# A split-float matmul kernel: high products of both halves first, then the low products of both halves

## What is computed

```python
def second_block(x, ...):
    for layer in range(2):
        if layer == 0:                                   # chunked attention with a relative bias
            h = rms_norm(x, a_norm)
            q, k, v, g = split(h @ a_w_in, 4)
            o = chunked_relbias_attention(q, k, v, a_rel_bias)
            x = x + (o * silu(g)) @ a_w_out
        else:                                            # attention with cumulative log forget gates
            h_kv = rms_norm(x, kv_norm)
            k, v = split(h_kv @ kv_w, 2)
            decay = cumsum(log_sigmoid(h_kv @ f_w + f_b))
            q, g = split(rms_norm(x, b_norm) @ b_w_in, 2)
            o = forgetting_attention(q, k, v, decay)
            x = x + (o * silu(g)) @ b_w_out
    return rms_norm(x, final_norm)
```

## Time and profile before

| | us | |
|---|---|---|
| median of three runs | 2486.72 | 2486.25 to 2486.83 |
| the profiled execution | 2486.6 | its span is 2484.9 |
| recurrence and what is ahead of it | 0 to 487.8 | TensorE busy 470.6 |
| output projection | 487.8 to 579.4 | TensorE busy 91.1 |
| layer 0 and layer 1 | 579.4 to 2430 | TensorE busy 1849.5 of 1850.6 |
| last projection and norm | 2430 to 2484.9 | TensorE busy 46.4 |

### The profile page before, as it was taken

One profiled execution on the slowest core, in us unless ns is written; L12 is line 12 of the kernel. 1 busy time (PEld: TensorE's weight loads), 2 busy tenths in 40 slices (PEclk: granted clock), 3 DMA queues, 4 the chain that ended last, 5 costly groups with the idle time before them and its releaser, 6 DMA issues.

```text
span 2484.9 us, 43962 instructions
## 1 busy us (share of the span) xinstructions
PE 2457.6 (99%) x16586; PEld 2187.6 (88%) x16586; DVE 1754.9 (71%) x2629; ACT 1219.4 (49%) x1811; POOL 304.0 (12%) x397
## 2 busy tenths in 40 slices
PE   8999999999999999999999999999999999999998
PEld 7999999888888888888888888888888888888887
DVE  8988797996767566666666668667576756666676
ACT  6555333665544444444534456544444444444445
POOL 1212114422100000000000001111010001000011
PEclk9999999999999999999999999999999999999999
DMA  7666763486576666666666665767667766766673
GB/s 216 173 160 170 196 183 87 111 225 189 162 193 187 191 175 181 184 173 193 175 193 186 175 174 167 194 186 185 191 171 190 193 184 182 189 180 181 189 194 102
DMA packets 758308, 442.79 MB, mean 178 GB/s; under 512 B 28784, under 2 KB 721136, under 8 KB 758160
## 3 DMA queue, kind: packets, MB, share of 16 engines
q1 hardware_dynamic: 752880, 430.16, 61.8%
q0 software_dynamic: 5280, 10.56, 3.2%
HBM read 437.35 MB, written 3.31 MB: 177 GB/s over the span
## 4 chain that ended last, share of the span: by engine, by line
PE 95%; DVE 3%; issue 1%; DMA 0%; ACT 0%; POOL 0%; SPq 0%; DVEq 0%; ACTq 0%
PE bank L288 40%; PE bank L294 20%; PE bank L269 5%; PE bank L270 5%; PE bank L271 5%; PE bank L318 5%; PE bank L319 5%; PE bank L320 5%; PE bank L1851 1%; PE bank L1870 1%; PE bank L1858 1%; PE bank L1850 1%; PE bank L1871 1%; DVE lob L253 0%; DMA rawa<-in_w_in_dram 0%
## 5 line engine op out<-in xcount | busy, mean ns | idle before, releaser
L253 DVE TENSOR_TENSOR lob<-rawb,hib 128x1024 fp32r<-128x1024 f32 x672 | 834.6, 1256 | 377.1 <-ACT hib L246 371.0
L246 ACT ACTIVATE hib<-rawb 128x1024 fp32r<-128x1024 f32 x672 | 701.4, 1055 | 515.5 <-PE bank L294 368.0
L288 PE MATMUL bank<-xx,hib 128*128 128x512 f32 x3328 | 842.7, 395 | 0.5 <-DVE xx L2126 0.3
L288 PEld LDWEIGHTS bank<-xx,hib 128*128 128x128 f32 x3328 | 601.5, 189 | 110.5 <-DVE xx L2126 0.9
L294 PEld LDWEIGHTS bank<-xx,lob 128*128 128x128 f32 x3328 | 459.8, 190 | 32.8
L294 PE MATMUL bank<-xx,lob 128*128 128x256 f32 x3328 | 487.3, 285 | 0.0
L269 PE MATMUL bank<-xh,hia 128*128 128x258 f32 (+2 forms) x1040 | 301.7, 290 | 10.7 <-DVE loa L253 10.5
L270 PE MATMUL bank<-xl,hia 128*128 128x258 f32 (+2 forms) x1040 | 296.5, 285 | 0.0
L271 PE MATMUL bank<-xh,loa 128*128 128x258 f32 (+2 forms) x1040 | 295.8, 284 | 0.0
L288 PE MATMUL bank<-oo,hib 128*128 128x512 f32 x1008 | 256.7, 393 | 0.0
L269 PEld LDWEIGHTS bank<-xh,hia 128*128 128x128 f32 x1040 | 197.3, 190 | 15.6 <-DVE loa L253 10.7
(11 more groups left out here) (294 smaller groups left out, 2260.4 us busy)
## 6 DMA issues: line engine op xcount, KB each, us to landing
rawb<-in_a_w_in_dram SPq DMA_DIRECT2D x256, 512.0 KB, 4.7
rawa<-in_w_in_dram SPq DMA_DIRECT2D x130, 512.0 KB, 5.4
rawb<-in_kv_w_dram SPq DMA_DIRECT2D x128, 512.0 KB, 4.5
rawb<-in_b_w_in_dram SPq DMA_DIRECT2D x128, 512.0 KB, 5.2
rawb<-in_a_w_out_dram SPq DMA_DIRECT2D x64, 512.0 KB, 5.1
rawb<-in_b_w_out_dram SPq DMA_DIRECT2D x64, 512.0 KB, 5.0
rawb<-in_w_out_dram SPq DMA_DIRECT2D x32, 512.0 KB, 4.8
table<-in_rel_dram POOLq DMA_DIRECT2D x32, 128.0 KB, 4.0
```

The source lines that it names most:

```text
L246: nc.scalar.activation(self.hi[(2 * at.u + h) % SPL][:], self.raw_half(at, h), ACT.Copy).then_inc(hi_ready, 1)
L253: nc.vector.tensor_tensor(self.lo[b][:], self.raw_half(at, h), self.hi[b][:].bitcast(F32), ALU.subtract).then_inc(lo_ready, 1)
L288: nc.tensor.matmul(out, self.hi[b][:, k * P:(k + 1) * P], both(k).rearrange("p a t -> p (a t)"), start=start and k == 0, stop=False)
```

## The change

`product_wide` and `wide`, which work through one half (8 high products, then 8 low ones), become `pair_wide`, which takes both halves of a unit: the high products of half 0, those of half 1, the low products of half 0, those of half 1. `half_used` is counted up after each half's low products, as before. All wide units go through it: the output projection of the first block, q, k and g of every head, and the projections, where the wait for the bank's last use (`taken`) is made once for both halves. The places of the attention work are written anew. In q_b and k_b it stood before the first high tile of half 1 and now stands before high tile 4 of half 1; in g_a and g_b it stood before low tile 3 of half 0 and now stands before high tile 1 of half 1; the second weighing stood before low tile 3 of half 1 and now stands before low tile 2 of it. In the first unit of each projection the wait for the neighbouring bank stays ahead of half 1's first high tile, which now comes right after six high tiles of half 0. The very last unit keeps its order.

```diff
-        def product_wide(self, pe, at, h, out, both, start, stop, tiles=range(8), before={}):
-
-            b = (2 * at.u + h) % SPL
-            pe.wait_ge(hi_ready, at.count(2 * at.u + h + 1, 2))
-            for k in tiles:
-                if ("hi", k) in before:
-                    before["hi", k]()
-                nc.tensor.matmul(out, self.hi[b][:, k * P:(k + 1) * P], both(k).rearrange("p a t -> p (a t)"),
-                                 start=start and k == 0, stop=False)
-            pe.wait_ge(lo_ready, at.count(2 * at.u + h + 1, 2))
-            for k in tiles:
-                if ("lo", k) in before:
-                    before["lo", k]()
-                last = nc.tensor.matmul(out[:, 0:SEQ], self.lo[b][:, k * P:(k + 1) * P], both(k)[:, 0], start=False,
-                                        stop=stop and k == 7)
-            if k == 7:
-                last.then_inc(half_used, 1)
+        def pair_wide(self, pe, at, outs, both, starts, stops, tiles=range(8), before={}):
             for h in range(2):
+                b = (2 * at.u + h) % SPL
+                pe.wait_ge(hi_ready, at.count(2 * at.u + h + 1, 2))
+                for k in tiles:
+                    if ("hi", h, k) in before:
+                        before["hi", h, k]()
+                    nc.tensor.matmul(outs[h], self.hi[b][:, k * P:(k + 1) * P], both(h, k).rearrange("p a t -> p (a t)"),
+                                     start=starts[h] and k == 0, stop=False)
+            for h in range(2):
+                b = (2 * at.u + h) % SPL
+                pe.wait_ge(lo_ready, at.count(2 * at.u + h + 1, 2))
+                for k in tiles:
+                    if ("lo", h, k) in before:
+                        before["lo", h, k]()
+                    last = nc.tensor.matmul(outs[h][:, 0:SEQ], self.lo[b][:, k * P:(k + 1) * P], both(h, k)[:, 0],
+                                            start=False, stop=stops[h] and k == 7)
+                if k == 7:
+                    last.then_inc(half_used, 1)
+
+        def unit_wide(self, pe, at, xx, before={}):
+
+            wait(pe, taken[at.bank()], at.free())
+            self.pair_wide(pe, at, [GB[at.bank()]] * 2, lambda h, k: xx[:, 8 * h + k], (True, False), (False, True),
+                           before=before)
...
-                for h, (n, rows) in enumerate(out_parts(v)):
-                    if (v, h) == (2, 0):
-                        pe.wait_ge(turned_taken, 2 * (NT - 1))
-                        turn_last()
-                    before = {}
+                at, tiles = out_unit(v), out_parts(v)
+                if v == 2:
+                    pe.wait_ge(turned_taken, 2 * (NT - 1))
+                    turn_last()
+                if tiles[0][0] >= EARLY:
+                    wait(pe, taken[at.bank()], at.free())
+                before = {}
+                for h, (n, rows) in enumerate(tiles):
                     if rows is rows_a:
-                        pe.wait_ge(ya_low, 1)
-                        before = {("hi", 4): lambda: pe.wait_ge(xlo_ready, 2)}
-                    a_first = CT if rows is rows_a else 0
-                    if n < EARLY:
-                        st.product_wide(pe, out_unit(v), h, out_bank(n), lambda k: xx[1][:, a_first + k], rows is rows_b,
-                                        rows is rows_a, before=before)
-                    else:
-                        st.wide(pe, out_unit(v), h, out_bank(n), lambda k: xx[1][:, a_first + k], rows is rows_b,
-                                rows is rows_a, before=before)
+                        before["hi", h, 0] = lambda: pe.wait_ge(ya_low, 1)
+                        before["hi", h, 4] = lambda: pe.wait_ge(xlo_ready, 2)
+                first = [CT if rows is rows_a else 0 for n, rows in tiles]
+                st.pair_wide(pe, at, [out_bank(n) for n, rows in tiles], lambda h, k: xx[1][:, first[h] + k],
+                             [rows is rows_b for n, rows in tiles], [rows is rows_a for n, rows in tiles], before=before)
...
-                        st.unit_wide(pe, q_b, xq, ({}, {("hi", 0): scores(j_a, q_a, k_a)}))
-                        st.unit_wide(pe, k_b, xk, ({}, {("hi", 0): turn_probs(j_a)}))
-                        st.unit_wide(pe, g_a, xg, ({("lo", 3): both(scores(j_b, q_b, k_b), weigh(j_a))}, {}))
-                        st.unit_wide(pe, g_b, xg, ({("lo", 3): turn_probs(j_b)}, {("lo", 3): weigh(j_b)}))
+                        st.unit_wide(pe, q_b, xq, {("hi", 1, 4): scores(j_a, q_a, k_a)})
+                        st.unit_wide(pe, k_b, xk, {("hi", 1, 4): turn_probs(j_a)})
+                        st.unit_wide(pe, g_a, xg, {("hi", 1, 1): both(scores(j_b, q_b, k_b), weigh(j_a))})
+                        st.unit_wide(pe, g_b, xg, {("hi", 1, 1): turn_probs(j_b), ("lo", 1, 2): weigh(j_b)})
 
                 def project(g):
-                    def product(at, half, tiles):
-                        if is_last(g) and layer == 1 and m == GH - 1:
-                            st.product(pe, at, half, psum[2 * at.bank() + half][:, 0:SEQ], lambda k: oo[:, k, 0],
-                                       lambda k: oo[:, k, 1], start=True, stop=True, tiles=tiles)
-                            return
-                        st.wide(pe, at, half, psum[2 * at.bank() + half], lambda k: oo[:, k], start=True, stop=True,
-                                tiles=tiles)
+                    def products(at, tiles, before={}):
+                        st.pair_wide(pe, at, [psum[2 * at.bank() + half] for half in range(2)], lambda h, k: oo[:, k],
+                                     (True, True), (True, True), tiles=tiles, before=before)
                     for m in range(GH):
                         at = place(layer, g, n=m)
+                        wait(pe, taken[at.bank()], at.free())
                         if m == 0:
                             other = at + -1
                             pe.wait_ge(ol_ready, head_no(layer, g, 0, GH - 2))
-                            product(at, 0, range(0, 6))
-                            pe.wait_ge(taken[other.bank()], other.evacuated())
-                            product(at, 1, range(0, 6))
+                            products(at, range(0, 6), {("hi", 1, 0): lambda: pe.wait_ge(taken[other.bank()],
+                                                                                       other.evacuated())})
                             for head in range(GH - 2, GH):
                                 pe.wait_ge(ol_ready, head_no(layer, g, 0, head + 1))
-                                for half in range(2):
-                                    product(at, half, range(head, head + 1))
+                                products(at, range(head, head + 1))
+                        elif is_last(g) and layer == 1 and m == GH - 1:
+                            for half in range(2):
+                                st.product(pe, at, half, psum[2 * at.bank() + half][:, 0:SEQ], lambda k: oo[:, k, 0],
+                                           lambda k: oo[:, k, 1], start=True, stop=True)
                         else:
-                            for half in range(2):
-                                product(at, half, range(8))
+                            products(at, range(8))
```

More of the change, by code:

```diff
@@ L299, in unit_wide @@
-        def unit_wide(self, pe, at, xx, before=({}, {})):
-            for h in range(2):
-                self.wide(pe, at, h, GB[at.bank()], lambda k: xx[:, 8 * h + k], start=h == 0, stop=h == 1,
-                          before=before[h])
+        def pair_wide(self, pe, at, outs, both, starts, stops, tiles=range(8), before={}):
+            for h in range(2):
+                b = (2 * at.u + h) % SPL
[15 more added lines that the diff above has]
+                    last.then_inc(half_used, 1)
```

## The result

The changed kernel took 2611.26 us (median of 6, 2604.51 to 2614.71) against 2486.89: a ratio of 1.0496 [1.0486, 1.0507], or +124.4 us. The forecast was 2587 in a range of 2550 to 2608. The sign and four fifths of the size were right; the time lies 3 us above the range. The profiled execution took 2604.51, the lowest of the six, so it shows 118 of those 124 us.

A forecast was written before the change was run, and what follows sets the result against it. TensorE, busy 99% of the span, was taken to bound the kernel. Pair stalls 83.8, first projection units 7.2, starting again 10.4, output projection 0.9 and gain -2.0 summed to +100.3 us: 2587, range 2550 to 2608.

The forecast's parts named there:

- The k_b stall, 2.05: k_b's transposes wait for softmax shares queued behind a split that needs q_b's half 0: 2.05 us in each of 32 pairs.
- The scores, 0.35: In g_a, scores wait for k_b's evacuation, queued behind a low part that needs k_b's half 0: 0.35 us per pair.
- g_b's transposes, 0.22: In g_b, transposes wait for the second head's scaling, behind a split that needs g_a's half 0: 0.22 us per pair.
- The projection, 0.9: First projection unit's half 1 waits for g_b's evacuation: 0.7 to 1.0 us, taken as 0.9, 8 times, 7.2 us.
- B + 4.75: Counted from g_b's start B: ScalarE's next pair of splits, at B + 5.03 at the latest, 4.75 if the waits overlap.
- The output projection, 0.19 + 0.9: At the output projection's start, unit 6 already waits 0.19 us for VectorE; about 0.9 us more reaches it, once.
- The gain, -2: Fewer changes between high and low products in 271 units save between 0 and 5 us; taken as -2.
- Starting again, 10.4: Refilling TensorE's pipeline after each of 104 stalls costs 0.10 us: 10.4 us, bounds 0 and 14.6.
- rival (b): Clock falls to half after the 2 us stall, k_b's remaining tiles take twice as long: 90 us more, 2677; chance 0.04.
- (a): Only the k_b stall shows, since the other engines catch up while TensorE waits: +67, 2553; chance 0.07.
- (c): Cover holds because the maxima do not stand behind the split of g_a's half 0: 2482 to 2485; chance 0.07.

The follow-up runs named there:

- The three kernels of the table without a fall: Changed kernel with k_b's transposes moved later (stall 1.13 or 1.6 us), or its 2.05 us stall filled with useless products: 2562.93, 2576.76, 2591.8 us.
- the last two kernels: Changed kernel with queues reordered, old order in output units 0 to 6 and first projection unit: 2487.5 us; kernel before with those queue orders only: 2490.19 us.
- all_but_last: Changed kernel with softmax of head a, evacuation of k_b and softmax of head b each ahead of a second split in the queues: 2491.33 us, 1.0017.
- the filled one: Changed kernel with eight useless 512-column products ahead of the transposes in k_b: 2591.8 us, 1.0415.
- softmax_first: Changed kernel with the softmax of head a ahead of q_b's second split on VectorE and ScalarE: 2521.01 us, 1.0131.

## Why the prediction was right and where it was wrong

**The k_b stall, 2.05.** Right: transposes predicted 4.81 after k_b's start, 4.80 in the trace, and each row of the chain within 0.02 of its forecast. The three kernels of the table without a fall give 31 us per us of stall.

**The scores, 0.35, and g_b's transposes, 0.22.** Right in place: 2.42 against 2.42, and 2.27 against 2.29. The list of waits has less idle time (7.0 in 25 for the scores, and one wait for g_b's transposes); it counts from modelled ends.

**The projection, 0.9.** 6.9 / 8 = 0.86. The working has a slip: from B + 4.75 it comes to B + 8.86, not 9.0, so the stall was 0.6 to 0.9 and not 0.7 to 1.0. **The output projection, 0.19 + 0.9.** 1.1. **The gain, -2.** -2.7, inside 0 to -5; shown by the last two kernels.

**Starting again, 10.4.** Somewhat low. An undisturbed pair takes 39.75 us, and 36.74 in the same order without the stalls (all_but_last): 3.01, of which the three stalls are 2.62 by the forecast. That leaves 0.39 for starting again three times, 0.13 each where 0.10 was taken, inside the bound of 0.14. Without falls of the clock the whole is 104.9 against 100.3 (103.6 against the kernel before that ran beside the filled one); some 3 of the 3 to 5 us over are this term's, and a single one is the 33rd wait of L1854, where g_b's transposes of one pair in the first group wait 1.3 us.

**The step that failed is the clock: the sum has no term for it, because rival (b) was dismissed.** It was set up as all or nothing, every k_b at half clock for 90 us or none, and put aside at 0.04 because "the stall here is shorter and dense work stands on both sides". Both are true and neither excludes it: the clock fell behind stalls of about 2 us between dense stretches, in 11 pairs of one execution. Its price by fall was mis-sized as well: 2.8 us was put on each, 1.1 to 1.3 was measured, for the half clock ends some 3.4 us after it began, before k_b's last low tiles are through (sixteen took 2.65 us instead of 2.06, not twice as long), and where a pair falls the scores in g_a wait less (0.08 us in the mean of 11 pairs, against 0.29 in the other 21). Times 32 pairs, that error made the rival look like 2677 and far away, when the mixed case adds 11 x 1.15 = 13 us to the profiled execution and 19.5 to the median. The Trainium skill spoke for this ("TensorE: Matmul & The Clock Gate", section "HAM oscillation — how this bites in real kernels"), as the prediction said; the runs agree with it in part: the falls are there, in some rounds of the loop and not in every round. The prediction left out that the gaps of which the section speaks are longer than this stall, so the Trainium skill did not by itself make the case 2677; that falls come behind 2 us is what these runs show.

With 19.5 us for the clock the sum would have been 2607, and the remaining 4 are those of the paragraph before.

**The other rivals.** (a) fell with the softmax_first run. (c) fell with the trace itself: the maxima do stand behind the split of g_a's half 0.

## What to carry to other kernels

When products are reordered, list what each buffer's release moves by, and follow it through the strict order of the engines behind it to whatever stands there waiting its turn: 1.84 us of later release cost nothing at the splits themselves, whose result is due a unit later, and 2 us at the softmax queued behind one of them. The remedy was one entry of a queue, not the order of the products; but each chain moved ahead uncovers another, so follow the last entry too.

Price a new stall of TensorE twice, as its length and as a chance that the clock falls behind it, and let the second be a share of the rounds, not all or none. Filling the stall with useless work, as here, tells the two prices apart.

## What the runs showed of the hardware that was not expected

- The clock fell to 0.50 behind a stall of about 2 us with dense work on both sides, in 11 (0.991 for the span) and 17 (0.987) of 32 pairs, behind 2.75 us in 19 (0.985), behind 1.6 and 1.1 in none, and once behind 1.79. After stalls of about 2 us each fall held for some 3.4 us and cost 1.1 to 1.3 us. The runs of the kernel after spread over 10 us (2604.51 to 2614.71), those of the filled one over 2 (2590.35 to 2592.63). Of equal stalls some were followed by a fall and some were not, and the falls of an execution keep a rhythm that the stalls do not set; what sets it is open.
- Useless work on TensorE in place of a stall made the kernel faster, by 19.5 us for 32 x 1.84 us of products.
- Two of VectorE's splits of 128x1024 took 3.74 us instead of 2.48 while GpSimd worked on 64x64 and then on 128x512; beside its 64x64 operation alone (1205.86) they took 2.48. That GpSimd is the cause was not isolated.
